# Peer stage, down phase: 64 of 256 tokens by indexed rows on VectorE, 64 packed as one weight

## What is computed

```python
eidx = jnp.take_along_axis(cidx, pos, axis=-1)          # (t, 8 heads, 16): i1 * 128 + i2
g = jax.nn.softmax(best, axis=-1)
act = jax.nn.gelu(jnp.einsum('thkd,td->thk', u[eidx], hb).astype(jnp.float32), approximate=False)
return jnp.einsum('thk,thkd->td', (g * act).astype(hb.dtype), v[eidx])
```

## Time and profile before

| | |
|---|---|
| time, median of 3 executions | 2027.77 us (2027.01 to 2029.61) |
| span of the profiled execution | 2025.5 us (its time outside the span is not given) |
| TensorE busy | 2012.9 us, 99% |
| GpSimd busy | 1559.7 us, 77% |
| ScalarE busy | 1147.4 us, 57% |
| VectorE busy | 1123.0 us, 55% |
| DMA moved | 395.29 MB, 195 GB/s on average |

### The profile page before, as it was taken

One profiled execution on the slowest core, in us unless ns is written; L12 is line 12 of the kernel. 1 busy time (PEld: TensorE's weight loads), 2 busy tenths in 40 slices (PEclk: granted clock), 3 DMA queues, 4 the chain that ended last, 5 costly groups with the idle time before them and its releaser, 6 DMA issues.

```text
span 2025.5 us, 39146 instructions
## 1 busy us (share of the span) xinstructions
PE 2012.9 (99%) x15608; PEld 1901.2 (94%) x15608; DVE 1123.0 (55%) x2110; ACT 1147.4 (57%) x1952; POOL 1559.7 (77%) x866
## 2 busy tenths in 40 slices
PE   9999999999999999999999999999999999999998
PEld 9999999999999979999889999999999998888886
DVE  6866745555454475224854316997788524444445
ACT  7344874445434486444654545557887655555555
POOL 5999789998999658898766677798777794444443
PEclk9999999999999999999999999999999999999999
DMA  9665456666666524665444454355444556555563
GB/s 353 218 217 187 167 188 250 219 219 247 251 249 224 205 92 154 239 231 203 177 169 146 167 188 178 133 191 174 164 165 167 167 187 208 189 196 194 191 217 127
DMA packets 80357, 395.29 MB, mean 195 GB/s; under 512 B 11084, under 2 KB 12236, under 8 KB 52176
## 3 DMA queue, kind: packets, MB, share of 16 engines
q1 hardware_dynamic: 80064, 393.24, 55.0%
q10 hardware_dynamic: 144, 0.04, 0.0%
HBM read 392.19 MB, written 1.05 MB: 194 GB/s over the span
## 4 chain that ended last, share of the span: by engine, by line
PE 89%; POOL 5%; issue 2%; DVE 2%; ACT 1%; DMA 1%; SPq 0%; ACTq 0%; POOLq 0%; DVEq 0%
PE bank L543 28%; PE bank L544 27%; PE bank L545 27%; POOL ring_low L496 5%; PE bank L1064 2%; PE bank L2845 1%; PE bank L2846 1%; DMA ring_raw<-in_stream 1%; PE bank L1857 1%; ACT ring_high L478 0%; PE bank L1886 0%; PE bank L1913 0%; PE bank L2861 0%; POOL peerS_low L2803 0%; DVE nsa_SB L2115 0%
## 5 line engine op out<-in xcount | busy, mean ns | idle before, releaser
L496 POOL TENSOR_TENSOR ring_low<-ring_raw,ring_high 128x1024 fp32r<-128x1024 f32 (+1 forms) x408 | 1027.3, 2549 | 186.9 <-ACT ring_high L478 185.3
L2803 POOL TENSOR_TENSOR peerS_low<-peerS_raw,peerS_high 128x512 fp32r<-128x512 f32 x384 | 498.3, 1316 | 241.1 <-ACT peerS_high L2958 240.4
L543 PE MATMUL bank<-keep_xThigh,ring_high 128*128 128x256 f32 x2080 | 582.0, 280 | 0.7 <-DVE keep_xTlow L3148 0.5
L544 PE MATMUL bank<-keep_xTlow,ring_high 128*128 128x256 f32 x2080 | 576.3, 277 | 0.0
L545 PE MATMUL bank<-keep_xThigh,ring_low 128*128 128x256 f32 x2080 | 576.3, 277 | 0.0
L478 ACT ACTIVATE ring_high<-ring_raw 128x2048 fp32r<-128x2048 f32 x204 | 390.2, 1913 | 257.8 <-PE bank L545 237.7
L543 PEld LDWEIGHTS bank<-keep_xThigh,ring_high 128*128 128x128 f32 x2080 | 390.7, 188 | 4.8 <-issue 2.9
L544 PEld LDWEIGHTS bank<-keep_xTlow,ring_high 128*128 128x128 f32 x2080 | 391.8, 188 | 0.3
L545 PEld LDWEIGHTS bank<-keep_xThigh,ring_low 128*128 128x128 f32 x2080 | 390.8, 188 | 0.0
L2958 ACT ACTIVATE peerS_high<-peerS_raw 128x512 fp32r<-128x512 f32 x508 | 319.3, 630 | 110.6 <-PE bank L545 105.8
L543 PE MATMUL bank<-keep_xThigh,peerS_high 128*128 128x256 f32 x1024 | 287.8, 281 | 0.3 <-POOL peerS_low L2803 0.3
(11 more groups left out here) (572 smaller groups left out, 3877.5 us busy)
## 6 DMA issues: line engine op xcount, KB each, us to landing
ring_raw<-in_stream SPq DMA_DIRECT2D x214, 1024.0 KB, 4.8
peerS_raw<-in_experts SPq DMA_DIRECT2D x254, 512.0 KB, 3.6
modcols_w<-in_ada_cols SPq DMA_DIRECT2D x32, 512.0 KB, 5.8
modlate_w<-in_ada_cols SPq DMA_DIRECT2D x8, 512.0 KB, 5.6
modcols_rows<-in_cond_rows SPq DMA_DIRECT2D x3, 1024.0 KB, 8.4
ring_raw<-in_stream SPq DMA_DIRECT2D x4, 512.0 KB, 7.3
keep_x<-in_x SPq DMA_DIRECT2D x2, 512.0 KB, 6.2
context_in<-in_ctx SPq DMA_DIRECT2D x1, 1024.0 KB
```

The lines of the kernel that those rows point to most:

```text
L496: self.nc.gpsimd.tensor_tensor(low_[:, cut], self.raw_slot(n)[:, cut], high[:, cut].bitcast(F32), ALU.subtract).then_inc(done.sem, 1)
L543: mm(out, sh, mh, start=start, stop=False)
L544: mm(out, sh, ml, start=False, stop=False)
L2803: g_.tensor_tensor(low[:, m % 2, cut], raw_of(m)[:, cut], high[:, m % 2, cut].bitcast(F32), ALU.subtract).then_inc(made_low.sem, 1)
```

## The change

The tokens are divided in three: 128 main tokens (0 to 127), 64 *packed* ones (128 to 191), and 64 *picked* ones (192 to 255).

- **Main tokens** are multiplied as before, three matmuls per column half.
- **Packed tokens**: one weight of 128 columns holds the 64 high halves and beside them the 64 low halves. It is multiplied with the high and the low half of `v`: two matmuls per column half, all four partial products. Each token's sum then lies in two places (PSUM partitions 0 to 63 and 64 to 127), added at the end. A tile takes 2 x (3 + 2) = 10 matmuls.
- **Picked tokens** leave the dense form after the gelu. Their gelu values are put in an SBUF buffer by one more ScalarE instruction per tile, and SyncE writes them to a DRAM tensor (`aside`), 256 KB every 8 tiles. After the selection VectorE works out, for each picked token and pick, the row number in `experts` and the place in `aside` (`index_picked`, 11 instructions). With 64 tokens x 128 picks laid over 128 partitions, there are 64 picks per partition. In the down phase GpSimd issues 64 indexed DMAs of 128 single values from `aside` and 64 indexed DMAs of 128 rows of 4 KB from `experts`, and VectorE adds each row times its share into a sum in PSUM (`pick(i)`, one 128x1024 instruction). The picks lie at tiles 8 to 118, four in every seven tiles; a row is asked for five tiles ahead.
- The quads go from 64 to 48 (192 tokens). All other work on A is 192 columns wide.
- `split_low` becomes two instructions (64 and 128 columns); the split activations get three slots.
- GpSimd makes the left low halves from the eighth down tile on, as before; for tiles 2 to 7 VectorE makes both.
- From the seventh down tile on, raw loads have six slots, not three.
- The end runs in the order token half 1 (packed and picked), then 0, over the last three tiles. ScalarE moves the packed tokens' upper partitions, VectorE adds them.
- All eight PSUM banks become one tensor; the counters of the earlier stage are freed early in this one.

The core of the diff:

```diff
+        DENSE, PICKED, CHUNK = 192, 64, 8
+        QUADS = DENSE // 4
+        PICKS = PEER_HEADS * PEER_TOPK // 2
...
+        SHARED, FIRST_PICK, LAST_PICK = N + 2, 8, 120
+        pick_at = lambda i: FIRST_PICK + 7 * i // 4
+        rows_at = lambda n: [i for i in range(PICKS) if pick_at(i) - 5 == n]
+        def places_at(n):
+            first = {3: range(0, 4), 4: range(4, 8)}
+            return first.get(n, [i for i in range(8, PICKS) if pick_at(i - 8) - 1 == n])
+        def left_on_dve(m):
+            n = m - N
+            return m >= SHARED and (n < FIRST_PICK or False)
...
+                c = (m - 4) // CHUNK - 1
+                if 0 <= c < N // CHUNK and (m - 4) % CHUNK == 0:
+                    sp.wait_ge(*gelued.at(CHUNK * (c + 1)))
+                    sp.dma_start(aside[:, CHUNK * c:CHUNK * (c + 1), :], apart[:, c % 2]).then_inc(aside_here[c % 2].sem, 16)
...
+                if m == N + 3:
+                    pool.wait_ge(*shared.at(1))
+                    for b in range(2):
+                        pool.wait_ge(*aside_here[b].at(16 * N // CHUNK // 2))
+                for i in places_at(m - N):
+                    if i >= 16 and i % 8 == 0:
+                        pool.wait_ge(*shared.at(i // 8))
+                    g_.indirect_dma_start(acts[:, i:i + 1], None, aside.rearrange("p n (t o) -> (p n t) o", o=1),
+                                          bass.IndirectOffsetOnAxis(place_of[:, i:i + 1], 0)).then_inc(acts_here[i // 8 % 2].sem, 16)
+                for i in rows_at(m - N):
+                    if i >= 4:
+                        pool.wait_ge(*row_used.at(i - 3))
+                    g_.indirect_dma_start(rows[i % 4], None, experts.rearrange("n p (h d) -> (n p h) d", h=2),
+                                          bass.IndirectOffsetOnAxis(row_of[:, i:i + 1], 0)).then_inc(row_here[i % 4].sem, 16)
...
+                    main(n, h, n == 0, False)
+                    packed(n, h, n == 0, False).then_inc(used.sem, 1)
...
+                s_.activation(apart[:, c % 2, n % CHUNK, :], ps[n % 2][:, DENSE:T], ACT.Gelu).then_inc(gelued.sem, 1)
...
+            def pick(i):
+                if i % 8 == 0:
+                    share_acts(i // 8)
+                dve.wait_ge(*row_here[i % 4].at(16 * (i // 4 + 1)))
+                if i == 0:
+                    ins = v_.tensor_scalar(picked_sum, rows[0], share[:, 0:1], None, ALU.mult)
+                else:
+                    dve.wait_ge(*row_used.at(i))
+                    ins = v_.scalar_tensor_tensor(picked_sum, rows[i % 4], share[:, i:i + 1], picked_sum, ALU.mult, ALU.add)
+                ins.then_inc(row_used.sem, 1)
 
             for n in range(2, N):
                 split_low(n)
                 if n < N - 1:
-                    low_half_of(N + n)
+                    if left_on_dve(N + n):
+                        low_half_of(N + n, 0)
+                    low_half_of(N + n, 1)
+                for i in picks_at(n):
+                    pick(i)
```

More of the change, by code:

```diff
@@ L2687, in peer, with raw_place, raw_of @@
         SCALE, LOW_ACT = 2.0 ** 14, 3
-        GA = [side(f"GA{n}", 2 * T, dt=F32R).rearrange("p (b t) -> p b t", b=2) for n in ("high", "low")]
+        GA = side("GA", 3 * 2 * DENSE, dt=F32R).rearrange("p (b t) -> p b t", b=3)
         iota = side("iota", P)
[L2690 to L2693, removed]
+        cell = lambda n: GA[:, n % 3, :]
+        MAIN_HIGH, PACKED, MAIN_LOW = slice(0, P), slice(P, 2 * P), slice(2 * P, 3 * P)
+        after = Arena(nc, "peerA", a_at, self.keep)
+        A = after("A", N * DENSE).rearrange("p (n t) -> p n t", t=DENSE)
+        rows = [after(f"row{i}", D) for i in range(4)]
+        raw_more = [after(f"raw{i}", D) for i in range(2)]
+        after.at = self.ring_end + 32 * 1024 + 46 * 1024 + 64
+        apart = after("apart", 2 * CHUNK * PICKED).rearrange("p (b n t) -> p b n t", b=2, n=CHUNK)
+        row_of, place_of = (after(name, PICKS, dt=U32) for name in ("row_of", "place_of"))
+        acts, share = after("acts", PICKS), after("share", PICKS)
+        token = after("token", 8)
+        raw_more.append(apart.rearrange("p b n t -> p (b n t)"))
+        aside = nc.dram_tensor("aside", [P, N, PICKED], F32, kind="Internal").ap()
         last_tile = Arena(nc, "peerL", a_at, self.keep)("last", 2 * D, dt=F32R).rearrange("p (s n) -> p s n", s=2)
         last_raw = Arena(nc, "peerLR", a_at + 8192, self.keep)("raw", 2 * D).rearrange("p (s n) -> p s n", s=2)
-        raw_of = lambda m: xraw[:, m % 3, :] if m < 2 * N - 2 else last_raw[:, m % 2, :]
+        DEEP = N + 7
+        def raw_place(m):
+            if m < DEEP:
+                return m % 3, m // 3
+            s, c = (m - DEEP) % 6, (m - DEEP) // 6
+            return (s, DEEP // 3 + c) if s < 3 else (s, c)
+        def raw_of(m):
+            if m >= 2 * N - 2:
+                return last_raw[:, m % 2, :]
+            s = raw_place(m)[0]
+            return xraw[:, s, :] if s < 3 else raw_more[s - 3]
         halves_of = lambda m, part: last_tile[:, part, :] if m == 2 * N - 1 else (high, low)[part][:, m % 2, :]
@@ L2853, in down, with main, packed @@
                     pe.wait_ge(*low_made(m, h))
[L2854 to L2857, removed]
+                    main(n, h, n == 0, False)
+                    packed(n, h, n == 0, False).then_inc(used.sem, 1)
+            def main(n, h, start, stop):
+                return self.product(ps[4 + h][:, :], [cell(n)[:, part] for part in (MAIN_HIGH, MAIN_LOW)],
+                                    [halves_of(N + n, i)[:, h * 512:(h + 1) * 512] for i in range(2)], start, stop)
+            def packed(n, h, start, stop):
+                for i in range(2):
+                    last = nc.tensor.matmul(ps[6 + h][:, :], cell(n)[:, PACKED], halves_of(N + n, i)[:, h * 512:(h + 1) * 512],
+                                            start=start and i == 0, stop=stop and i == 1)
+                return last
             for k in range(KD):
@@ L2927, in _ @@
             pe.wait_ge(*xcopied.at(4))
-            for n in range(N - 2):
+            for n in range(N - 3):
                 down(n)
-            pe.wait_ge(*gal.at(N))
-            for t in range(TT):
+            for t in ORDER:
                 for h in range(2):
[L2933 to L2939, removed]
+                    for n in (N - 3, N - 2, N - 1):
+                        if t == 1:
+                            if h == 0:
+                                pe.wait_ge(*gal.at(n + 1))
+                            pe.wait_ge(*(last_low.at(h + 1) if n == N - 1 else low_made(N + n, h)))
+                        last = (main, packed)[t](n, h, False, n == N - 1)
                     last.then_inc(banked.sem, 1)
```

207 lines of the change are left out of this document (141 added, 66 removed).

## The result

The changed kernel takes 2036.7 us (median of 4 runs, 2036.0 to 2038.1), the kernel before 2027.4 in the same comparison: ratio 1.0044, interval 1.0033 to 1.0056. It is slower, where 1992 us and faster were forecast. The profiled execution has a span of 2036.3 us, 10.8 more than before.

A forecast was written before the change was run, and what follows sets the result against it. TensorE, busy for 99% of the span, was taken as the bound, GpSimd as setting the down phase's pace after the change. 2025.5 - 58.0 - 7.6 + 26.2 + 3 + 0.5 = 1989.6, plus 2.3: 1992 us, range 1960 to 2060.

The forecast's parts named there:

- c: GpSimd's price for issuing one indexed DMA in the down phase: taken as 0.9 us, range 0.45 to 1.15.
- the start of the gathers: As the down phase begins: 4 us for the write, then 12 gathers in 10.8 us, before 18.1 us: costs nothing.
- the last tiles: End of the down phase: tiles at TensorE's 2.26 us in the last nine; final additions cost 0.5 us.
- TensorE and the quads: Fewer down-phase matmuls at 0.2264 us each save 58.0 us; 16 fewer quads, 8 pairs, save 7.6 us.
- the index work: VectorE's 11 instructions between selection and transposed results: 0 to 7 us reach TensorE, 3 taken.
- GpSimd's pace: Main case, tiles 8 to 118: lows, gathers and collisions take 2.50 us per tile, costing 26.2 us; chance 0.40.
- Its sign: Down phase, in the changed profile: TensorE waits on GpSimd's low half, GpSimd has no gaps between tiles 8 and 118.
- The slower rival: Down phase: GpSimd's gathers cost more than TensorE gives back, from 1.18 us each; 2068 us at 1.5; chance 0.30.
- Collisions: Down phase: GpSimd and VectorE hold each other up reading SBUF; 0.17 us per tile added to GpSimd.
- DMA hidden: Down phase: loads and gathers take 2.2 us of DMA per tile and cost nothing.
- The rule weighed in the prediction: Down phase: VectorE's two-SBUF-input work and GpSimd's SBUF reads never overlap: 2.46 us per tile, 313.3 us.
- some 1.10 us of a low half: Down phase: only this part of GpSimd's low half excludes VectorE, so both engines' work fits into 2.264 us.

The follow-up runs named there:

- no_gathers: Changed kernel without all but the first 4 row gathers and first 8 value gathers, picks reusing those rows: 1981.4 us, ratio 0.9771 to the kernel before.
- short_pick: Changed kernel with 63 of the 64 picks adding only 64 of the 1024 columns: 2039.0 us, ratio 1.0057 to the kernel before.
- order: Changed kernel with only the order of ScalarE's and VectorE's work in the down phase altered: 2045.1 us, ratio 1.0081 to the kernel before.
- two_slots: Changed kernel with ScalarE splitting a tile's weights only when the tile two before is used up: 2036.6 us, ratio 1.0045 to the kernel before.
- share3: Changed kernel with VectorE also making the left low half in 3 of 7 tiles, eighth to 119th: 2017.9 us, ratio 0.9954 to the kernel before.
- start: Changed kernel with four row gathers before GpSimd's wait, VectorE making left lows to the 13th down tile, picks from tile 12: 2033.1 us, ratio 1.0018.
- small_rows: Changed kernel with row gathers moving 1 KB per partition in place of 4 KB, same instructions: 2035.3 us, ratio 1.0035 to the kernel before.
- all_dve: Changed kernel with VectorE making every left low half up to the 119th tile: 1984.0 us, ratio 0.9786 to the kernel before.
- no_values: Changed kernel without the value gathers from the ninth to the 64th and their multiplications: 1986.3 us, ratio 0.9799 to the kernel before.
- start_all_dve: Changed kernel with the edits of both `all_dve` and `start`: 1980.2 us, ratio 0.9767 to the kernel before.

## Why the prediction was wrong

The shortfall lies in the down phase, 364.6 - 316.0 = 48.6 us of it, by stretch: the first eight tiles +1.0, the 2.3 tiles after them 18.1 for 5.8 (+12.3), the 105.1 tiles 290.0 for 262.8 (+27.2), the last 12.6 tiles 37.4 for 29.4 (+8.0). Three terms of the sum failed: the size of c, the start of the gathers, and the last tiles.

- **TensorE and the quads: right.** 0.2264 us a matmul wherever nothing is late (`no_gathers`), and two up tiles with a pair still take 6.40 us. With the index work the down phase begins 5.6 us earlier; 7.6 - 3 = 4.6 was forecast.
- **GpSimd's pace: the right mechanism, the wrong size.** c was taken as 0.9 us, two instructions of the nearest row; it is 0.98 and a gap of 0.17 before it, which no row of before could show: 111.3 / 97 = 1.15, the upper end of the prediction's own range. With that its sum gives 2.79 us per tile, and 2.82 were measured up to 1940. That alone would have been 2024, about no change. Its sign, TensorE waiting for GpSimd's low half, did not show in the long stretch of the changed kernel, where the wait names VectorE; it showed in `short_pick` and `order`. The slower rival named the right engine, but its price, c from 1.18, was not reached: what the time lies above 2024 is in the start and the last tiles, both put at nothing.
- **Collisions.** They were put on GpSimd at 0.17 us per tile. GpSimd's lows grew by only 0.03 (112.7 / 85 = 1.33 us for 1.30); VectorE's first piece of the split took the loss, 1.22 us in the mean where 0.20 was reckoned. Making that piece shorter brought nothing by itself (`two_slots`), nor did taking work from VectorE (`short_pick`). What the prediction did not see is that the term grows with VectorE's two-input work: to 0.48 us a low half in `share3` (92.5 us for 52, 1.78).
- **"Starting the gathers: nothing": the step that failed outright.** The write was there at 9.2 us, not at 4, and 12 gathers took 16.5 us, not 10.8; so the low half was late, TensorE stood 8.1 us, and it came back at the lower clock. `start` shows that little of this comes back while GpSimd is the bound. So the 12.3 and the 27.2 do not simply add: GpSimd has one amount of work to get through.
- **The last tiles at TensorE's pace: wrong by 8 us.** After 2010 TensorE is busy for 13.9 of 17.4 us at a clock of 0.90, with the three instructions that fold the picked sum (1.24 us each) between the last splits. GpSimd is not the cause here: from the 116th tile to the end the changed kernel takes 37.9 us and `no_gathers` 37.4, where 13 tiles at TensorE's pace are 29.4 (the rows below). That it is the three folding instructions is argued, not shown: no run takes them away.
- **DMA hidden: right** (`small_rows`). 2.2 us per tile were forecast; in `all_dve` a share of 0.98 of 2.29 us is 2.24. But `no_values`, without most of the value gathers, has the same share at the same pace, so these cost about nothing and the bytes more than reckoned. DMA is then nearly full; whether it would be the next bound no run shows.

From the 116th tile to the end, the changed kernel and `no_gathers`:

```profile
1989.50:2027.40 37.90, 33.03 (x131) 24.88 (x129) 31.02 (x52) 21.53 (x45) 15.57 (x12) 0.95 0.26 90
1933.80:1971.20 37.40, 32.76 (x131) 24.79 (x129) 30.71 (x50) 21.59 (x43) 15.37 (x12) 0.95 0.23 74
```

The rule weighed in the prediction, the Trainium skill's SBUF — State Buffer (Who interferes with whom), was reckoned to give 2.46 us per tile without any gather, and `no_gathers` shows 2.264. What fails is the sum, not the rule. GpSimd and VectorE in that run:

```profile
1747.68 1.29 POOL L2863 TENSOR_TENSOR peerS_low<-peerA_raw,peerS_high 128x512 fp32r<-128x512 f32 x1 [0.96 <-ACT peerS_high L3040]
1747.89 1.36 DVE L3323 TENSOR_TENSOR peerS_GA<-peerA_A,peerS_GA 128x64 fp32r<-128x64 f32 x2 [0.28 <-ACT peerS_GA L3082]
1749.18 0.68 DVE L3347 TENSOR_TENSOR peerS_low<-peerA_raw,peerS_high 128x512 fp32r<-128x512 f32 x1
1749.95 1.30 POOL L2863 TENSOR_TENSOR peerS_low<-peerA_raw,peerS_high 128x512 fp32r<-128x512 f32 x1 [0.98 <-ACT peerS_high L3040]
```

The split begins 0.21 us into the low half, and its first piece ends only 0.08 us after it. From the low half's end to the end of VectorE's last two-input instruction 0.89 us pass, not 1.16, because each of these begins shortly before the instruction ahead of it, the low half included, has ended. So the two engines' work, one after the other, takes 1.30 + 0.89 = 2.19 us and fits into 2.264, and the trace of `no_gathers` agrees with the rule. That only some 1.10 us of a low half exclude, as the prediction read the earlier trace rows, is not borne out.

The Trainium skill's same section says that VectorE can keep a GpSimd DMA from its descriptors, but that `tensor_tensor` did not do so in its probe. Here it does: in `all_dve` gathers took up to 3.63 us beside VectorE's `tensor_tensor`, and the measurement decides. These gathers read their places from SBUF; whether that is the reason no run shows.

The changed kernel moved 58 us of work off TensorE, and spent it on the one engine that had 0.96 us per tile to spare, 8 x 1.15 / 7 = 1.31 us per tile. With the left low halves on VectorE and the earlier start (`start_all_dve`) GpSimd's gathers are hidden in the long stretch, and the change is worth 47 us.

## What to carry to other kernels

Price an indexed DMA on its issuing engine at what it holds that engine, gap included, before its bytes: here 1.15 us for 128 entries, 4 bytes or 4 KB alike. When two engines hold each other up, the one that a wait names may be the victim: relieve each alone, and believe the one that brings the time back. A stall ahead of a stretch with another bound brings little when removed (`start`: 4 to 5 us of 8); mend the bound first.

## What the runs showed of the hardware

- An indexed DMA of 128 entries holds GpSimd 0.94 us at best, whatever the size of its rows (4 bytes: 0.976 in the mean of the changed kernel, 4 KB: 0.975; 1 KB in `small_rows`: 0.976), with a gap of about 0.15 to 0.30 us before it.
- VectorE's instructions with two SBUF inputs hold up GpSimd's making of such a DMA: means of 0.98 us in the changed kernel, 1.38 and 1.81 in `all_dve`, up to 3.63 there. The DMA did not hold up these instructions (0.69 us a low half in `all_dve`), and a VectorE instruction with one input in PSUM did not hold up the DMA (13 cases, 0.94 to 0.95 us).
- GpSimd's low half and VectorE's instructions with two SBUF inputs hold each other up. In `no_gathers` all 105 of these that began during a low half ended after it, 0.08 us in the median; in `share3`, with more of them, the low halves got longer (1.76 us for 1.34).
- TensorE's granted clock was 0.50 in the 8 us after a stand of 8.1 us, and 0.94 in the stretch with many short waits; at 1.00 the time was no better (`short_pick`).
